# Split-precision two-block transformer kernel: norms by token block and group of four column blocks, the first products of each section by token block, the gate's 8 columns moved into the latent product

## The reference, cut to what matters

```python
for l in range(2):                                   # first kind: "mix" and "ffn"
    h = rms_norm(x, g_mix[l]);  proj = h @ w_in[l]   # glu, indexer, attention, short conv, gates
    merged = sum(gates[b] * (y_b @ w_o[b]) for b in the four branches)
    x = x + merged @ w_merge[l]
    h2 = rms_norm(x, g_ffn[l])
    x = x + (silu(conv3(h2 @ w_ffn_gate[l])) * (h2 @ w_ffn_up[l])) @ w_ffn_down[l]
for l in range(2):                                   # second kind: "two"
    h = rmsnorm(x, norm_w[l]);  proj = h @ w_in_2[l] # 3752 columns
    # latent attention (416 columns), gated delta rule (q, k, v, z, and 8 columns b, a),
    # block attention (q, k, v, gate)
    x = x + concat(y_mla, y_gdn, y_moba) @ w_out[l]
out = rmsnorm(x, final_norm_w)
```

## Time and profile before

| | before |
|---|---|
| median of 3 runs | 1327.03 us (1326.93 to 1329.15) |
| time of the profiled execution | 1327.21 us |
| its span | 1325.4 us |
| TensorE busy | 1301.4 us (98%) |
| VectorE busy | 1026.0 us (77%) |
| ScalarE busy | 746.5 us (56%) |
| read from memory | 220.88 MB |

### The profile page before, as it was taken

The page is one execution under the profiler, slowest core; times in us unless marked ns, Lnnn a source line. Parts: engine busy times, 40 slices in busy tenths (PEclk is TensorE's granted clock), DMA queues, the critical chain, the costliest instruction groups (busy, mean ns, idle before and its releaser), DMA issues. The chain is left out here.

```text
span 1325.4 us, 26400 instructions
## 1 busy us (share of the span) xinstructions
PE 1301.4 (98%) x10796; PEld 1240.3 (94%) x10796; DVE 1026.0 (77%) x1763; ACT 746.5 (56%) x1149; POOL 47.3 (4%) x48
## 2 busy tenths in 40 slices
PE   9999999999999999999999999999999999999997
PEld 8899999999999999999999989999989899888996
DVE  6899998677777677999997768777778746677565
ACT  6544566556454465544757556544567445586364
POOL 0000000000000000100000000000001100001100
PEclk9999999999999999999999999999999999999999
DMA  8565455565555465646365555665654223343232
GB/s 279 190 201 181 160 161 189 163 220 186 196 191 191 153 229 176 215 162 197 126 210 167 197 184 178 207 203 193 206 163 152 64 97 128 122 143 112 81 101 75
DMA packets 108991, 223.62 MB, mean 169 GB/s; under 512 B 6180, under 2 KB 17700, under 8 KB 108872
## 3 DMA queue, kind: packets, MB, share of 16 engines
q1 hardware_dynamic: 106736, 218.99, 49.5%
q10 hardware_dynamic: 2136, 2.96, 0.7%
HBM read 220.88 MB, written 1.06 MB: 167 GB/s over the span
## 5 line engine op out<-in xcount | busy, mean ns | idle before, releaser
L1191 ACT ACTIVATE whi<-ring 128x1024 fp32r<-128x1024 f32 (+3 forms) x430 | 433.7, 1027 | 343.2 <-PE bank L513 221.3
L1764 DVE TENSOR_TENSOR wlo<-ring,whi 128x1024 fp32r<-128x1024 f32 (+3 forms) x430 | 496.9, 1180 | 166.0 <-ACT whi L1191 133.1
L513 PE MATMUL bank<-hhi,whi 128*128 128x256 f32 x2016 | 272.5, 277 | 2.5 <-ACT hhi L1228 1.8
L522 PE MATMUL bank<-hhi,wlo 128*128 128x256 f32 x2016 | 273.0, 277 | 1.0 <-DVE wlo L1764 1.0
L513 PE MATMUL bank<-hlo,whi 128*128 128x256 f32 x2016 | 269.1, 276 | 0.0
L513 PEld LDWEIGHTS bank<-hhi,whi 128*128 128x128 f32 x2016 | 248.3, 192 | 5.5 <-issue 3.9
L522 PEld LDWEIGHTS bank<-hhi,wlo 128*128 128x128 f32 x2016 | 246.9, 192 | 4.9 <-issue 3.2
L513 PEld LDWEIGHTS bank<-hlo,whi 128*128 128x128 f32 x2016 | 247.3, 193 | 0.0
L1932 DVE SCALAR_TENSOR_TENSOR w<-w,par 128x256 f32<-128x256 f32 x240 | 98.1, 479 | 0.0
L535 PE MATMUL bank<-whi,hhi 128*128 128x512 f32 (+2 forms) x256 | 93.1, 366 | 0.0
L535 PE MATMUL bank<-whi,hlo 128*128 128x512 f32 (+2 forms) x256 | 92.6, 364 | 0.0
(11 more groups left out here) (311 smaller groups left out, 1549.1 us busy)
## 6 DMA issues: line engine op xcount, KB each, us to landing
ring<-in_w_in SPq DMA_DIRECT2D x100, 1024.0 KB, 5.1
ring<-in_w_ffn_down SPq DMA_DIRECT2D x22, 1024.0 KB, 5.1
ring<-in_w_ffn_gate SPq DMA_DIRECT2D x20, 1024.0 KB, 5.1
ring<-in_w_ffn_up SPq DMA_DIRECT2D x20, 1024.0 KB, 5.2
ring<-in_w_merge SPq DMA_DIRECT2D x8, 1024.0 KB, 5.2
ring<-in_w_out SPq DMA_DIRECT2D x8, 1024.0 KB, 5.0
ring<-in_w_oc SPq DMA_DIRECT2D x4, 1024.0 KB, 5.3
ring<-in_w_od SPq DMA_DIRECT2D x4, 1024.0 KB, 5.2
```

Source lines behind the costliest of these rows:

```text
L513: done = e.matmul(o, wh[:, k, cols(u)], paired(s_[:, k0 + k, :]), stop=False, skip_group_check=True, start=opens and k == 0 and s_ is sh a ...
L522: done = e.matmul(o, wl[:, k, cols(u)], paired(sh[:, k0 + k, :]), start=False, stop=closes, skip_group_check=True)
L1191: e.activation(part_of(whi, j), part_raw(j), ACT.Copy).then_inc(*up("hi.a"))
L1764: e.tensor_tensor(part_of(wlo, j), part_raw(j), part_of(whi, j), ALU.subtract).then_inc(*up("lo.v"))
```

## The change

- **Norm weights** are no longer columns of `par` but rows: `rowg` (128x1024) is filled from `norm_rows` by a DMA on ScalarE's queue after each norm (`next_rows`), and VectorE multiplies x by it before the scaling (`weigh`), except in the first norm, where the turned block is multiplied in its bank. `hhi` and `hlo` are then written 128x512 at a time.
- **Ends.** `last_pairs` takes the last two pairs of parts (four parts) token block by token block, and puts the turning of the next norm's block 0 (`turn_norm`) before its last eighth.
- **Beginnings.** `chans_first` runs the first group block by block: each product streams 128 columns of `hhi` and 128 of `hlo` of one token block side by side (`hboth`), into four banks instead of two, the high and the low result apart. Block 1 is turned inside part 3. The two results are added later by a ScalarE copy and a VectorE add of each bank (`glu_high`, `gate_high`, `kc_high`). All `awake` products but the first 13 go.
- **Second kind.** The 8 columns of b and a are moved next to the latent input's 416; `m0` streams 424 columns and is second; `ba`, `rows8`, their turning and the 32 KB load go. The order is kc, m0, qc, vc, cqk, cvg, mg, z. `TWO_PLAN` is written anew.
- The Toeplitz rows for the bias are loaded in the last `ffn` section instead of at the beginning of the second kind; the group after the first takes its banks from the other four; the squares go to `sgb`.

```diff
-TWO_IN = (("kc", 1184, 1696), ("ba", 2720, 2728), ("qc", 672, 1184), ("m0", 0, 416), ("vc", 1696, 2208),
-          ("cqk", 2728, 3240), ("cvg", 3240, 3752), ("mg", 416, 672), ("z", 2208, 2720))
+TWO_IN = (("kc", 1192, 1704), ("m0", 0, 424), ("qc", 680, 1192), ("vc", 1704, 2216),
+          ("cqk", 2728, 3240), ("cvg", 3240, 3752), ("mg", 424, 680), ("z", 2216, 2728))
-        "taps": [12, 20, 34],
-        "others": [28, 34, 41, 41, 53],
-        "decay": [10, 10, 11, 12],
-        "delta": [17, 18, 20, 20, 30, 30, 36, 37, 39, 41, 43, 46, 46, 48, 48, 50, 51, 52, 53, 54, 55, 62, 65, 66, 66],
-        "latent": [26, 29, 30, 34, 36, 37, 39, 43, 46, 53, 54, 65, 66],
-        "outs": [58, 66, 71, 71],
+        "taps": [12, 26, 32],
+        "others": [31, 34, 39, 39, 51],
+        "decay": [16, 16, 20, 22],
+        "delta": [26, 27, 29, 29, 32, 32, 35, 36, 37, 39, 41, 44, 44, 46, 46, 48, 49, 50, 51, 52, 53, 60, 63, 64, 64],
+        "latent": [18, 23, 25, 28, 34, 35, 37, 41, 44, 51, 52, 63, 64],
+        "outs": [56, 64, 69, 69],
...
+            def last_pairs(j, acc, pairs, tag, l, following):
+                for tb in range(2):
+                    for n, ((sh, sl), k0, ready) in enumerate(pairs):
+                        for nh in range(2):
+                            part = j + 2 * n + nh
+                            wh, wl = part_of(whi, part), part_of(wlo, part)
+                            if tb == 0:
+                                e.wait_ge(SEM["hi.a"], part + 1)
+                                if nh == 0:
+                                    e.wait_ge(*at(*ready))
+                            elif n == 1 and nh == 1 and following:
+                                turn_norm(*following, 0)
...
+            def chans_first(j, held_of, name, l, mid, after):
+                def products(i, tb, blocks_):
...
+                            done = e.matmul(held[u][:, tb * S:tb * S + S], wh[:, k, cols(u)], hboth[:, :, 2 * i + k, cols(tb)],
+                                            start=i == 0 and k == 0 and tb == 0, stop=False, skip_group_check=True)
...
+                for i in range(4):
+                    e.wait_ge(SEM["hi.a"], j + i + 1)
+                    e.wait_ge(*at("hlo", name, l, 0, i // 2))
+                    products(i, 0, (0, 1))
+                    if i == 3 and not begins:
+                        turn_norm(name, l, 1)
+                    products(i, 0, (2, 3))
+                for i in range(4):
+                    e.wait_ge(*at("hlo", name, l, 1, i // 2))
+                    products(i, 1, range(4)).then_inc(*up("first.p"))
+                    mid(j + i)()
+                    low_ready(j + i)
...
+                            done = e.matmul(sides(held[u])[0], wl[:, k, cols(u)], two(hhi[:, 2 * i + k, :]), start=False,
+                                            stop=i == 3, skip_group_check=True)
...
-                bk = ps.take(e, "s", "gsum", l)
-                awake(bk, 6)
+                bk = ps.take(e, "s", "gsum", l)
...
+            def norm_a(name, l, x_in, j0):
+                square_a(name, l, x_in, 0)
+                split_to(j0 + 2)
+                high_a(name, l, 0, 0)
+                high_a(name, l, 0, 1)
+                square_a(name, l, x_in, 1)
+                split_to(j0 + 3)
+                scale_a(name, l, xn)
+                high_a(name, l, 1, 0)
+                high_a(name, l, 1, 1)
...
+                for nh in range(2):
+                    add(0, nh)
+                    weigh(0, nh)
                 sums_v(name, l, 0)
+                for g in range(2):
+                    scale_v(name, l, 0, g, xn)
+                split_to(j0)
+                add(1, 0)
+                low_v(name, l, 0, 0)
+                add(1, 1)
+                low_v(name, l, 0, 1)
                 sums_v(name, l, 1)
+                weigh(1, 0)
+                weigh(1, 1)
+                scale_v(name, l, 1, 1, xn)
+                split_to(j0 + 1)
+                low_v(name, l, 1, 0)
+                split_to(j0 + 2)
+                low_v(name, l, 1, 1)
```

More of the change, by code:

```diff
@@ L258, in split, with sides @@
             return ap.rearrange("p u (c s) -> p u c s", c=2)
+        def sides(bk):
+            return [bk[:, :].rearrange("p (t q s) -> p q t s", t=2, q=2)[:, q] for q in range(2)]
         def blocks(ap):
@@ L1102, in two_p @@
                 for name, _, _ in TWO_IN:
-                    if name == "ba":
-                        bk = ps.take(e, "m", name, l)
-                        wh, wl = part_of(whi, j), part_of(wlo, j)
-                        e.wait_ge(SEM["hi.a"], j + 1)
-                        for k in range(8):
-                            for s_ in (hhi, hlo):
-                                done = e.matmul(bk[0:8, 0:S], wh[:, k, :], paired(s_[:, k, :]),
-                                                start=k == 0 and s_ is hhi, stop=False)
-                        done.then_inc(*up("first.p"))
-                        low_ready(j)
-                        for k in range(8):
-                            done = e.matmul(bk[0:8, 0:S], wl[:, k, :], paired(hhi[:, k, :]), start=False, stop=k == 7)
-                        done.then_inc(*up("second.p"))
-                        j += 1
+                    if name == "kc":
+                        chans_first(j, lambda u: ps.take(e, "m", name, l, u), "two", l, between, behind)
+                        j += 4
                     elif name == "cvg":
@@ L2204, in ffn_v @@
                         last = [None] * 2
-                        e.wait_ge(*at("gpad", l, i6, i))
+                        if i6:
+                            e.wait_ge(*at("gpad", l, i6, i))
+                        else:
+                            for u in range(2):
+                                g2 = two(gpad[:, i, u, 2:258])
+                                e.wait_ge(*at("gate_high", l, 2 * i + u))
+                                e.tensor_tensor(g2, g2, sides(bank("gate", l, 0, 2 * i + u))[1], ALU.add).then_inc(*up("ffn.v"))
+                                leave("ffn.v", "gate", l, 0, 2 * i + u)
+                            e.wait_ge(*now("ffn.v"))
                         for k3 in range(3):
@@ L2537, in two_v @@
                         j += 1
+                    if name == "kc":
+                        for c in range(4):
+                            g2 = two(gdp[:, c // 2, c % 2, 3:259])
+                            e.wait_ge(*at("kc_high", l, c))
+                            e.tensor_tensor(g2, g2, sides(bank(name, l, c))[1], ALU.add).then_inc(*up("two.v"))
+                            put("two.v", "kc_sum", l, c)
+                            leave("two.v", name, l, c)
                     if name in ("kc", "qc", "vc"):
                         four_taps(l, ("kc", "qc", "vc").index(name), 0)
-                for i in range(6):
+                for i in range(4):
                     side.run(TWO_AT.get(2 * (j - two0(l)), ()))
```

471 lines of the change are left out of this document (255 added, 216 removed).

## The result

The changed kernel takes 1348.11 us (median of 4 runs, 1346.95 to 1350.01) against 1326.98 us (1325.01 to 1329.15) before: ratio 1.0161, 95% interval 1.0148 to 1.0174. It is 21 us slower where 19 us faster was forecast.

A forecast was written before the change was run, and what follows sets the result against it. TensorE, busy 1301.4 of 1325.4 us, was taken to set the time by its own sequence: 1327.2 - 6.0 (boundaries) - 11.4 (ba and decay) - 1.6 (latent steps) = 1308.2 us; range 1303 to 1313, over all 1301.5 to 1318.

The forecast's parts named there:

- The boundaries: Five section boundaries: 4.45 us between useful products becomes 3.25, a gain of 1.2 each, 6.0 for five.
- The beginning: Program's start: first product some 1.5 us sooner, two new waits of about 0.6 each; taken as 0, bounds -1 and +1.
- The plain reading: 576 products no longer read two halves alternately: taken as 0, other bound 60 us; rival that it is slow, 5%.
- What TensorE no longer does: Boundary fillers go; second kind, per layer: ba's 2.62 us, turnings 0.2 and gsum's fillers go, 0.16 us comes back.
- the one on decay: Ahead of gsum, second kind: fillers and wait of 2.29 and 2.78 us go; with the ba part 11.4 us together.
- the solve's later steps stand where they did: Second kind: the solve's later steps keep their places, counted in input parts; no size given.
- The wait on the rope: Turning of the latent keys, second kind: TensorE's wait goes, 1.6 us for both layers, bounds 0 and 1.6.
- side work was costed at nothing: VectorE's extra weighing and bank adds lie beside products, VectorE busy 77%: 0; without cover, adds about 2 us a norm.
- The rival of a slower TensorE: After each boundary, without fillers, TensorE runs at half speed: 17.9 us lost, 1326 us in all; chance 4%.
- the last, a stall in the new order of the second kind: Some other stall, such as a split too late in the second kind's new order, eats all gain: 1330 us; 4%.

The follow-up runs named there:

- Experiment 4: The changed kernel with three places of the second kind's gates moved later and the solve's first four steps one place earlier: 1325.19 us, ratio to before 0.9992.
- experiment 10: The kernel before with only the second kind's half of the change, gates and solve at the places of Experiment 4: 1330.62 us, ratio 1.0031.
- experiment 2: The kernel before with only the second kind's half of the change (new input order and places, no ba, no fillers ahead of gsum): 1349.85 us, ratio 1.0174.
- experiment 5: The changed kernel with one number changed, the first step of the key's gate at place 17 in place of 12: 1348.74 us.
- experiment 11: Two of three shifted taps of each gate left out, output differs: changed kernel 1331.75 us, kernel before 1321.00, Experiment 4 1319.44.
- experiment 3: The changed kernel with products of no use put ahead of the waits in the second kind's sections: 1339.58 us, ratio to before 1.0101.
- experiment 7: Products of no use ahead of waits: first on Experiment 4 with gsum's reading, latent norm and BT0 moved, 1336.06 us; second on Experiment 4 at the decay's turning, 1327.44.
- the light kernel of experiment 4: The kernel of Experiment 4 with two of the three shifted taps of each gate left out, output differs: 1319.44 us, ratio to the full kernel before 0.9946.

## Why the prediction was wrong

*The boundaries* were right: 1.2 us forecast, 1.2 measured from mark to mark at each of the first four, with waits of 0.32 to 0.34 for `xn` (0.35 forecast) and 0.51 for `hlo` (0.8 forecast). That the totals agree so well is in part luck: the wait that was 0.3 us too long in the sum is made up by small losses elsewhere, among them some 0.2 us a section of the plain reading. Experiments 4 and 10 give 5.4 us for all of them, 6.0 were forecast. The beginning, taken as 0, came to 0.1. The granted clock stayed at 1.00 through every boundary, so that rival fell.

*The plain reading* was right: eight products take 0.91 us (1162.87 to 1163.78 above) against 0.89 in the kernel before, not 0.1 us more each. Over 576 products that is about 1.4 us.
```profile
1018.14 1.06 PE L522 MATMUL bank<-hhi,wlo 128*128 128x256 f32 x8
1019.03 1.06 PE L513 MATMUL bank<-hhi,whi 128*128 128x256 f32 x8
```

*What TensorE no longer does* was right: 17.8 us of work, where the sum dropped about 9 of fillers at the boundaries (14 records of 0.125 in each) and 8.3 in the second kind (`ba` 5.24, turnings 0.4, fillers 3.0, less 0.3). With before's own idle and slow time the span would be 1280.2 + 23.9 + 3.4 = 1307.5.

*The step that failed* is the one on decay: "so the wait goes and nothing stands in for it", with "the solve's later steps stand where they did, counted in input parts" behind it. Three things in it were not so.

First, it weighed the chain from the copy to `gv` (4 to 5 us; 4.6 measured) and not what stands ahead of the copy. The copy came 4.7 us after its products, behind the key's gate. I had counted the decay's own steps as a load on the splits, and not the gate's as a load on the decay. The result was a wait of 2.4 and 2.6 us in the two layers in place of none. This alone is not the loss: with that wait gone the time was the same (experiments 2 and 5).

Second, "where they did" holds only from the solve's ninth step on. Counted in input parts the first four moved back by 11 places and `BT0` by 4, while the decay begins 8 later: decay to `BT0` had places 10 to 30 and has 16 to 32, so the same work has less room. And the order in it turned round: the key's squares stood ahead of the query's gate (18 and 20) and now stand behind it (27 and 26), and the value's gate stood behind `BT0` (34 and 30) and now has the same place, 32. The waits on the squares, the latent query and `BT0` are 19.0 us of the 25.8. Experiment 4, which moves the gates behind, takes most of them away; which of its seven numbers did it was not measured. The wait on the rope was forecast to go, 1.6 us, and did.

Third, side work was costed at nothing from a mean of 77% for VectorE. In the stretch right behind the key's group it is busy for 9.8 of 10 us (the window from 980; 8.2 in the same window of the kernel before). With a third of the taps' work left, half of the loss is gone (experiment 11). VectorE isn't short of time over the whole stretch, though: from 970 to 1055 it is busy for 58 us, and for 67 in the kernel before. It is full where the steps pile up, and then stands idle with TensorE.

*The clock.* The rival of a slower TensorE had the right mechanism, a lower granted clock where fillers were dropped, at the wrong place and with the wrong trigger: not the boundaries, but behind the new waits, and 18.7 us in size. The rival that came nearest was the last, a stall in the new order of the second kind, with 4% and 1330: the place was right, the stall was not a late split, and the time is 18 us beyond it. How much of the slow time counts depends on who sets the pace: 8.5 us came back in the changed kernel's order (experiment 3), nothing in the better one (experiment 7).

*Left open.* Whether an order exists that gives the full gain with all of the side work in: six were tried, and the best is level with the kernel before. Why the light kernel of experiment 4 keeps 29 us idle was not pursued beyond the waits named. What each of the seven numbers of experiment 4 is worth by itself was not run, but for one. The boundaries with an undisturbed old second kind were not measured: both attempts brought waits of their own.

## What to carry to other kernels

When a group of products is dropped or moved, the side work between them loses cover: write down, for each result that the main engine asks for, everything that stands ahead of its producer in that engine's queue and what *those* instructions wait for, not only its own chain. A mean busy share says nothing about a stretch; take the windows around the moved steps. And split the main engine's time into work at full clock, idle and slow before judging: here a gain of 18 us was real and visible in the first, and lost twice over in the other two.

## What was not expected of the hardware

A wait of about 2.4 us was enough for the granted clock to fall to 0.50, and it stayed there for 3 to 10 us, most of them busy. In the kernel before, layer 1's wait of 1.28 us at `gsum` has such a fall behind it (0.50 from 1171 to 1174), layer 0's of 0.79 has none. Waits of 0.3 to 0.5 us at the boundaries never lowered it. At the program's beginning, where TensorE waits twice, for 0.5 to 1.7 us and for 0.8 to 0.9, one of the fourteen traces with the new beginning has a dip (the light kernel of experiment 4, 0.50 from 10 to 12 us); the changed kernel's has none with the same instructions there. The Trainium skill ("TensorE: Matmul & The Clock Gate", Part 1) has two levels, half and full, and an idle array at the lower one; windows that lie wholly in a dip agree, at 0.50.

Waiting is not all of it. In the kernel before TensorE was busy for all but 0.24 us of the two stretches below, and the clock fell at about 1023.9, less than 1 us behind the sixteen one-column products of the squares' sums (1021.22 to 1023.14; columns as above).
```profile
1020.00:1023.00 3.00, 2.76 (x25) 2.60 (x25) 1.91 (x7) 2.54 (x4) 0.94 (x2) 1.00 1.05 401
...
1024.00:1027.00 3.00, 3.00 (x16) 3.00 (x16) 1.83 (x2) 1.20 (x3) 1.23 (x1) 0.50 0.18 29
```
In experiment 7's second kernel the dips also follow those products (at 1020.50, dip from 1022), but with the lighter gate the kernel before has the same products and no dip there. What sets it off is not settled.
